# Two-block kernel, one core: modulation vectors by VectorE's dot products, an earlier place for the context's mixing, and the modulation blocks in ScalarE's DMA queue

## What is computed

```python
def _modulation(cvec, w_mod, b_mod):
    m = jax.nn.silu(cvec) @ w_mod + b_mod
    return jnp.split(m[:, None, :], 6, axis=-1)

def second_block(x, c, ctx, c_ctx, ...):
    for l in range(DEPTH):
        m_x = _modulation(c, w_mod[l], b_mod[l])
        m_c = _modulation(c_ctx[None, :], w_mod[l], b_mod[l])
        h = _modulate(x, norm1_g[l], m_x[0], m_x[1])
        hc = _modulate(ctx, norm1_g[l], m_c[0], m_c[1])
        ...
        x = x + m_x[5] * _peer(h2, ...)
        if not last:
            ctx = ctx + m_c[2] * mix_c
            ...
```

## Time and profile before

| | us |
|---|---|
| median of three runs | 3965.93 (3962.25 to 3976.16) |
| span of the profiled execution | 3961.4 |
| PE busy | 3596.4 (91%) |
| DVE busy | 2300.7 (58%) |
| ACT busy | 664.2 (17%) |
| POOL busy | 1284.5 (32%) |
| read from HBM | 1201.64 MB, 304 GB/s over the span |

### The profile page before, as it was taken

One profiled execution on the slowest core, in us unless ns is written; L12 is line 12 of the kernel. 1 busy time (PEld: TensorE's weight loads), 2 busy tenths in 40 slices (PEclk: granted clock), 3 DMA queues, 4 the chain that ended last, 5 costly groups with the idle time before them and its releaser, 6 DMA issues. The chain is left out here.

```text
span 3961.4 us, 41101 instructions
## 1 busy us (share of the span) xinstructions
PE 3596.4 (91%) x14600; PEld 2547.8 (64%) x14600; DVE 2300.7 (58%) x5460; ACT 664.2 (17%) x1814; POOL 1284.5 (32%) x1130
## 2 busy tenths in 40 slices
PE   8998999989999999999999989788779998877777
PEld 6667788878876888888847876333335786433333
DVE  3342013566877887765762147777763226777775
ACT  2232101110001330000002212111112211111111
POOL 1100000023445456774650013444341003444442
PEclk9999999999999999999999999899899999998999
DMA  8752345357998889998983259999996339999997
GB/s 331 291 202 89 128 149 191 128 207 291 345 354 343 292 296 412 406 400 343 414 353 132 102 221 411 398 414 407 411 419 274 108 126 375 405 419 419 420 419 327
DMA packets 206842, 1205.50 MB, mean 304 GB/s; under 512 B 23472, under 2 KB 24640, under 8 KB 95024
## 3 DMA queue, kind: packets, MB, share of 16 engines
q0 software_dynamic: 154976, 858.34, 54.0%
q1 hardware_dynamic: 51664, 344.55, 23.0%
HBM read 1201.64 MB, written 1.15 MB: 304 GB/s over the span
## 5 line engine op out<-in xcount | busy, mean ns | idle before, releaser
L1656 PE MATMUL bank<-big 128*128 128x256 f32 (+4 forms) x8888 | 1909.3, 374 | 47.3 <-DVE big L2435 13.8
L1656 PEld LDWEIGHTS bank<-big 128*128 128x128 f32 (+2 forms) x8888 | 1628.9, 190 | 338.3 <-issue 90.8
L2980 POOL DMA_INDIRECT big<-in_pboth,big x1024 | 1213.2, 1185 | 1301.0 <-PE bank L2134 703.7
L2134 PE MATMUL bank<-big 128*128 128x512 f32 x2048 | 990.6, 641 | 224.7 <-ACT big L2943 224.6
L2635 DVE CUSTOM_DVE_ANT_0 big<-big 128x1024 f32<-128x1024 f32 x768 | 926.1, 1223 | 338.6 <-DMA big<-in_pboth,big 333.2
L2134 PEld LDWEIGHTS bank<-big 128*128 128x128 f32 x2048 | 409.6, 204 | 785.8 <-issue 483.8
L2646 DVE SCALAR_TENSOR_TENSOR big<-big 128x1024 f32<-128x1024 f32 x254 | 326.1, 1284 | 75.7 <-DMA big<-in_pboth,big 55.3
L2967 POOL TENSOR_TENSOR big<-big 128x1 f32<-128x1 f32 (+1 forms) x49 | 42.4, 865 | 914.5 <-DVE big L2192 914.3
L2943 ACT ACTIVATE big<-big 128x128 f32<-128x128 f32 x512 | 165.4, 391 | 270.5 <-DVE big L2612 266.0
L2933 ACT ACTIVATE big<-big 128x4 f32<-128x4 f32 (+2 forms) x136 | 28.1, 207 | 730.9 <-DVE big L2608 725.6
L1836 PE MATMUL bank<-big 128*128 128x256 f32 x576 | 129.5, 378 | 0.0
(11 more groups left out here) (218 smaller groups left out, 2279.7 us busy)
## 6 DMA issues: line engine op xcount, KB each, us to landing
big<-in_w SPq DMA_DIRECT2D x104, 1024.0 KB
big<-in_wmod POOLq DMA_DIRECT2D x48, 1024.0 KB, 8.9
big<-in_wgu SPq DMA_DIRECT2D x44, 1024.0 KB
big<-in_wzg SPq DMA_DIRECT2D x36, 1024.0 KB, 4.8
big<-in_wro SPq DMA_DIRECT2D x32, 1024.0 KB
big<-in_wpq SPq DMA_DIRECT2D x24, 1024.0 KB, 4.9
big<-in_wd SPq DMA_DIRECT2D x22, 1024.0 KB
big<-in_pboth,big POOLq DMA_INDIRECT x1024, 11.0
```

What stands on the lines that cost most here:

```text
L1656: last = pe.matmul(o, a, b, start=(i == 0), stop=(i == n - 1))
L2134: last = pe.matmul(u.ap, d.ap, row[:, 512 * i:512 * i + 512], start=(k == 0), stop=(k == 127))
L2980: g.indirect_dma_start(out=s.ap, out_offset=None, in_=table, in_offset=bass.IndirectOffsetOnAxis(ap=index, axis=0)).then_inc(s.full[0], 16)
```

## The change

`modulation` is rewritten. The silu of c (or c_ctx) is laid out as a row, the same on all 128 partitions; w_mod is transposed on the host, so that a block of 128 outputs by 1024 inputs (0.5 MB) has one output on each partition; one DVE instruction multiplies it with the row and sums it, giving one column of `mcols`. c_ctx is done first (48 blocks of layer 0, 16 of layer 1), then c (96 blocks): 160 blocks. After eight blocks `mod_sixth` adds the bias and forms the gain; after 48, `mod_rows` turns the columns on PE and stores the rows.

The modulation is a third stream, "m", drawn with `MOD_PACE`; the context's stream begins its mixing as soon as 16 blocks are done, and other places draw from "m" where they need its results. Its slots are `mod_spare` (until the context's mixing is over), two in `MT` of the first block (until the first `merge`) and `mod_late` in `fw` (from there on). The blocks are asked for by ACT in place of POOL. The paces of the gathers are lower. Some small buffers are moved to make room. The core of the diff:

```diff
-PACES = (0.8, 1.8, 1.5, 0.79, 0.47, 0.73, 4.0)
+PACES = (0.8, 1.8, 1.5, 0.66, 0.41, 0.66, 4.0)
+MOD_PACE = 0.6
+MOD_END = 1024
...
-        self.streams(self.x_stream(ar), self.context_stream(), PACES[0])
+        self.mods_ok, self.sixths, self.cols_ok = {}, set(), None
+        self.mod_spare = Slot(self.big[:, BIG_N - MOD_END - 1024:BIG_N - MOD_END], self.sem("wm0"))
+        self.mod_ring, self.mod = Ring([self.mod_spare]), self.modulation()
+        self.streams(self.x_stream(ar), self.context_stream(), self.mod, PACES[0])
         self.put("finished", stored=(self.sem("d_out"), self.counts["d_out"]))
 
-    def streams(self, a, b, pace):
-        ta = tb = 0.0
-        live = {"a": a, "b": b}
+    def streams(self, a, b, m, pace):
+        ta = tb = tm = 0.0
+        live = {"a": a, "b": b, "m": m}
         while live:
             which = "b" if "b" in live and (tb <= ta * pace or "a" not in live) else "a"
+            if "m" in live and tm < ta * MOD_PACE:
+                which = "m"
...
-                for _ in live.pop("b", ()):
+                for _ in chain(live.pop("b", ()), live.pop("m", ())):
                     pass
+            elif which == "m":
+                tm += step
...
-        ar = Arena(self.big, self.B0, BIG_N - self.B0)
+        ar = Arena(self.big, self.B0, BIG_N - MOD_END - self.B0)
         few = [Slot(ar.get(2048), self.sem(f"wb{i}")) for i in range(2)]
         mark = ar.at
-        yield from self.modulation(self.pb, few, ar)
-        ar.at = mark
+        self.put("load_context")
+        self.tick("d_ctx", 16)
+        yield 16
+        while (0, 1, 1) not in self.sixths:
+            next(self.mod)
+            yield 2
         self.put("context_in")
         yield "pace", PACES[1]
+        ar.size -= 1024
         yield from self.mix_phase(self.pb, Ring(few), self.smallb, ar, 0, self.C, 1, False)
+        self.mod_moves([self.mod_spare], [])
+        while (0, 1, 5) not in self.sixths:
+            next(self.mod)
+            yield 2
         yield "pace", PACES[2]
-        yield from self.peer_c(self.pb, Ring(few), self.smallb, self.B0 + mark, BIG_N - self.B0 - mark, 9, 0, self.C)
+        yield from self.peer_c(self.pb, Ring(few), self.smallb, self.B0 + mark, BIG_N - MOD_END - self.B0 - mark, 9, 0, self.C)
...
+        mod_slots = [Slot(MT.rearrange("p a b -> p (a b)")[:, 1024 * i:1024 * i + 1024], self.sem(f"wm{i + 1}")) for i in range(2)]
+        mod_late = Slot(fw, self.sem("wm3"))
+        self.mod_ring.slots.extend(mod_slots)
...
+                for _ in self.mod:
+                    pass
+                for c in cv.slots:
+                    c.freed = mod_late.freed
...
+                mod_late.freed = cv.slots[cv.at % 2 - 1].freed
+                self.mod_moves(mod_slots, [mod_late])
+                put("mod_moved", ready=[w.freed for w in mod_slots])
...
-    def modulation(self, banks, few, ar):
...
-                for k in range(8):
-                    while srcs and len(coming) < 4:
-                        coming.append(self.load(wr, srcs.pop(0), 2048))
-                        put("mod_weights", w=coming[-1])
-                    w = coming.pop(0)
-                    done = tick("mod_part", 4)
-                    w.free(done)
-                    if k == 3 and late:
-                        part_end()
-                    put("mod", w=w, u=u, cc=cc, k=k, ready=(self.sem("mod_c_done"), 1) if l + part + k == 0 else None,
-                        done=done)
-                    yield 3
...
+    def mod_moves(self, gone, new):
+        self.mod_ring = Ring([w for w in self.mod_ring.slots if w not in gone] + new)
+        while any(w.freed == "held" for w in gone):
+            next(self.mod)
+
+    def mod_room(self):
+        ring = self.mod_ring
+        for _ in ring.slots:
+            if ring.slots[ring.at % len(ring.slots)].freed != "held":
+                return ring
+            ring.at += 1
+        return None
+
+    def modulation(self):
         put, tick, t = self.put, self.tick, self.t
-        c2, c3 = ar.get(16), ar.get(16)
-        bm = Ring([Slot(ar.get(512), self.sem(f"d_bm{i}")) for i in range(2)])
-        wr = Ring([Slot(ap, self.sem(f"wm{i}")) for i, ap in enumerate([w.ap for w in few] + [ar.get(2048) for _ in range(5)])])
-        st = Ring([Slot(ar.get(512)) for _ in range(2)])
-        put("load_context")
-        tick("d_ctx", 16)
-        put("mod_zero", parts=[s.ap for s in st.slots])
-        put("mod_c", c2=c2, c3=c3, loaded=tick("d_c2", 16), tanh=tick("mod_tanh"), done=tick("mod_c_done"))
-        cc = c3.rearrange("p (k v) -> p k v", k=8)
-        stored = [None, None]
-        srcs = [t["wmod"][l, part, k] for l in range(2) for part in range(3) for k in range(8)]
-        coming, late = [], []
-
-        def part_end():
-            l, part, args = late.pop()
-            put("mod_store", **args)
-            u = Use(banks.banks[(3 * l + part) % 2])
-            self.cols_ok = u.free
-            c4 = self.mcols[:, 2 * l:2 * l + 2, 16 * part:16 * part + 16].rearrange("p v (j b) -> p v j b", j=4)
-            gains = [(self.gcols[:, 4 * l + 2 * v + part // 2, :], self.mcols[:, 2 * l + v, 8 + 24 * (part // 2):16 + 24 * (part // 2)],
-                      self.col[l, "n2" if part else "n1"]) for v in range(2)] if part != 1 else []
-            put("mod_columns", src=args["rows"], u=u, ready=args["ready"], dst=c4, gains=gains)
-
-        yield 30
-        for l in range(2):
-            for part in range(3):
-                s, b, u = st.take(), self.load(bm, t["bmod"][l, part], 512), Use(banks.banks[(3 * l + part) % 2], full=False)
-                put("mod_bias", ws=[b])
-                for k in range(8):
-                    while srcs and len(coming) < 4:
-                        coming.append(self.load(wr, srcs.pop(0), 2048))
-                        put("mod_weights", w=coming[-1])
-                    w = coming.pop(0)
-                    done = tick("mod_part", 4)
-                    w.free(done)
-                    if k == 3 and late:
-                        part_end()
-                    put("mod", w=w, u=u, cc=cc, k=k, ready=(self.sem("mod_c_done"), 1) if l + part + k == 0 else None,
-                        done=done)
-                    yield 3
-                put("mod_add", u=u, b=b, s=s, summed=done)
-                b.free(u.free)
-                turn = (3 * l + part) % 2
-                stored[turn] = tick(f"d_st{turn}", 64)
-                s.free(stored[turn])
-                rows = self.mods[l].rearrange("v a d -> v (a d)")
-                late.append((l, part, dict(rows=s.ap, dst=[rows[:, 2048 * part + 512 * j:2048 * part + 512 * j + 512] for j in range(4)],
-                    src=[s.ap[32 * j:32 * j + 2, :] for j in range(4)], ready=u.free, done=stored[turn])))
-        part_end()
-        for w in few:
-            w.freed = done
-        self.mods_ok = list(stored)
-        self.c_ok, self.b_free = u.free, [u.free]
-        put("mods_stored", ready=self.mods_ok)
+        ar = Arena(self.big, BIG_N - MOD_END, MOD_END)
+        vector, sums = ar.get(1024), [self.small[:, 40 + 8 * i:48 + 8 * i] for i in range(2)]
+        put("load_mod_bias", dst=self.mcols, loaded=tick("d_bias", 16))
+        blocks = [(l, v, b) for v in (1, 0) for l in range(2) for b in range(16 if l and v else 48)]
+        left, coming, at, done = list(blocks), [], None, None
+        for l, v, b in blocks:
+            if v != at:
+                tmp, at = self.mod_room().take(), v
+                tmp.slot.count -= 16
+                ready = tick("mod_vector")
+                put("mod_c", dst=vector, tmp=tmp, src=t["crow"][v].to_broadcast([P, 1024]), before=done, loaded=tick("d_c2", 16),
+                    tanh=tick("mod_tanh"), done=ready)
+                tmp.free(ready)
+            while left and left[0][1] == v and self.mod_room():
+                l2, _, b2 = left.pop(0)
+                coming.append(self.load(self.mod_room(), t["wmod"][l2, b2], 1024))
+                put("mod_weights", w=coming[-1])
+            w, done = coming.pop(0), tick("mod_part")
+            w.free(done)
+            put("mod", w=w, vector=vector, to=sums[b // 8 % 2][:, b % 8:b % 8 + 1], done=done)
+            if b % 8 == 7:
+                part, j = b // 8, 2 * l + v
+                self.cols_ok = tick("mod_columns")
+                gain = None
+                if part in (1, 4):
+                    n = part // 4
+                    gain = (self.gcols[:, 4 * l + 2 * v + n, :], self.col[l, "n2" if n else "n1"])
+                put("mod_sixth", sums=sums[part % 2], ready=done, dst=self.mcols[:, j, 8 * part:8 * part + 8], gain=gain,
+                    biased=tick("mod_biased") if gain else None, done=self.cols_ok)
+                self.sixths.add((l, v, part))
+                if part == 5:
+                    s, u, self.mods_ok[l, v] = self.mod_room().take(), self.pb.take(), tick("d_mods", 16)
```

(111 more changed lines are left out.)

61 lines of the change are left out of this document (17 added, 44 removed).

## The result

The changed kernel takes 4211.5 us (median of four runs, 4208.1 to 4216.9), the kernel before 3964.6 us beside it: a ratio of 1.063 (95% interval 1.0605 to 1.0646), +247 us. The forecast was slower by 100, with a range up to 4125; the direction was right and the size was not.

What follows compares the result with a forecast made beforehand. PE was taken to set the pace of the first half, DVE following with slack: 3961.4 - 52 + 20 + 20 + 104 + 20 - 10 = 4063 us, 4068 as a median, taken as 4065; range 3920 to 4125.

Steps and rivals of the forecast that it cites:

- matmuls and turns removed: PE's path: 48 groups of modulation matmuls save 49 us, column turns 3 us, together -52 us.
- context sooner, slower paces: Context's mixing from about unit 30 beside x's dense work, and gathers spread over more units: -10 us.
- units 5 to 44, three slots: Early x units: PE starts some 6 us late and 25 blocks outpace DVE; +20 us (5 to 40).
- units 44 to 183, three slots: From unit 44 of x to the end of context's mixing: no term in the sum, nothing charged.
- units 183 to 257, two slots: After context's mixing, up to the first merge: 36 blocks, DVE 151 us against PE 133; +20 us (0 to 40).
- one slot: Units 257 to 304, 33 blocks in mod_late: DVE pays landing times; +104 us (40 to 180).
- SP's queue: SP waits for DVE at three places and loses x's prefetch each time: +20 us (0 to 45).
- after the first gather: From the first gather on: the sum has no added cost; after 2075 us nothing changes.
- DVE's slack would not cover the stalls: Against the faster rival, stalls covered by DVE's slack: 3914 us, between 3890 and 3954, chance 0.23.
- the run-ahead I had credited: One-slot stretch: PE can run ahead by four banks, some 15 us, subtracted within the +104.
- PE's busy time: Profile of the changed kernel: PE busy near 3545 us.
- The rival with ScalarE: ScalarE waiting in order for mod_part delays tanh and copies, and blocks land after 6 us: 4184 us, chance 0.10.

Runs made afterwards that it cites:

- the mended order: Changed kernel, no block before x's norm, rows three blocks later, vectors asked by GpSimd, early issue; without loads and products: 3954.5 us, ratio 0.9975.

## Why the prediction was wrong in size

| term | forecast | measured |
|---|---|---|
| matmuls and turns removed | -52 | about -38 (28 to 52; three quarters of 52, by the run with fewer columns) |
| context sooner, slower paces | -10 | about +40, small products included: without blocks the new order gives 0 in place of -38 |
| units 5 to 44, three slots | +20 | +19 by stretches |
| units 44 to 183, three slots | 0 | +55 by stretches (41 + 14) |
| units 183 to 257, two slots | +20 | +49 by stretches, with the lost clock |
| one slot | +104 | +117 by the run, 113 by stretches |
| SP's queue | +20 | +19 by the run; it lies within the other rows |
| after the first gather | 0 | 0 |

Without SP's term, which the other rows hold already, the measured column adds up to 242, for 247. The second row is a remainder and not a measurement: it rests on the -38 above it, and the run without blocks 2 to 91 shows that some 23 us of it go with those blocks.

- **What held.** The mechanism with the largest term, a ring of one slot on an in-order DVE: 4.7 us a block for 4.8. So did SP's queue, the cost of a product, nothing lost after the gather, and that DVE's slack would not cover the stalls. DVE waits 160.6 us for blocks, over the 150 named, and DVE's total of 2478 is near 2490.
- **The step that failed most** is a term that the sum doesn't have: between unit 44 and unit 183, with three slots and some 67 blocks, the forecast charged nothing and gave no reason. By stretches it cost 55 us (17 with the products alone, 29 with the loads alone), and the run without blocks 2 to 91 was 99 us faster where the forecast had 20. Waiting for blocks isn't what it was: DVE waited 29 us of 557 for them. DVE's slack was measured as idle share, but here the engine is idle because it waits for its turn in x's and the context's chains. A product, or an issue of ScalarE, that stands ahead of a chain's next step makes the chain longer. That is my reading of it; that either alone costs time is shown (+75 and +159 over all 160 blocks, DVE being busy only 57% of the time up to the gather in the first: 425 of 749 us), but no run shows how much of a single product's length a chain pays.
- **The sign of "context sooner"** was wrong. I took free places in PE's row as a gain from denser mixing; the trace without blocks shows PE idle 103 us before the gather, for 51. -10 became about +40, the second largest miss; part of it is the small products, and its own cause stays open.
- **The two-slot stretch** cost 49 us by stretches for 20.
- **PE's own new wait was missed.** I went through SP's, ScalarE's and DVE's queues, and not PE's turns at the end of each vector: 81.8 us in three waits, 64.0 in the last. It is the place where the one-slot loss appears rather than a loss of its own, and it ends the run-ahead I had credited (15 us). That would explain 104 against 117; no run took it out.
- **PE's busy time** should have been 3545 and is 3589. Up to the gather it is 614 us, where 790 - 170 - 52 gives 568: 46 us more (13 of them without any blocks, where it is 581). Stretches with many gaps were granted 0.68 to 0.85 of the clock, and this term stood nowhere in my sum.
- **The rival with ScalarE** named a true mechanism (ACT's copies up to 18.3 us late) and a wrong price: undone, it gives 13 us, as DVE stands behind it and GpSimd's blocks land later. Its total of 4184 came near by adding other terms, not by this one.
- **The first gather** came at 920 us, for 770 forecast, and block one ended at 2322, for 2175: 150 and 147 late, the same error as in the total (146).
- **One reading was off**, without weight in the sum: the first two DMA slices that the new loads fall on read 8 and 7, and not 2 to 5.

The Trainium skill (DMA: Bandwidth & Descriptors, "Rules for kernel authors") asks to issue early and wait late. These runs agree in that DVE waited 28.8 us for the first 91 blocks, with three slots, and 87.4 us for the last 33, with one; and with one slot issuing right behind the product gained nothing (5.4 us a block in GpSimd's queue with it and without it). Its rule that issuing engines are no queues of their own ("Issuing engines are not separate DMA queues") fits the totals: ScalarE's queue in place of GpSimd's gave no time in either kernel (+13 and +11 us). It doesn't fit each transfer, where by that rule only issue time is saved: issuing took 0.33 us for 0.53, landing 3.7 us for 4.3 in the median, and a block of the one-slot stretch 4.7 us for 5.4.

Open stays the order's cost of about 40 us beyond the 11 that the mended order gave back and the part that is the small products', and the two-slot stretch by a run of its own.

## What to carry to other kernels

An engine's idle share is not room. Ask for each piece put on a "free" engine which chain's next step stands behind it in that queue, and charge the piece's full length, as an upper bound, where the chain is what ends last; a ring of one slot costs product plus landing for each block. Walk through every queue for new waits, the bounding engine's own first, and add what gaps cost in granted clock.

## What the runs showed of the hardware

- A stalled PE pays twice: its same 261 records took 54.4 us at a granted clock of 1.00 and 62.3 us at 0.68, 15% more, besides the gaps.
- A transfer of 0.5 MB in ScalarE's queue landed after 3.7 us in the median over 160, 3.2 at least and 11.4 at most, while SP's loads ran too; in the first 112 us the median was 4.6, for the 5 to 6 that I took there. In GpSimd's queue the same 160 took 4.3 us in the median.
- With one slot a block took 4.7 us in ScalarE's queue and 5.4 in GpSimd's, 1.3 of it product.
- Taking 28.7 us of matmuls from a row that shows PE busy without a gap gave 21 us, 16 to 28 by the interval.
